# Expert input rows gathered in quarters and turned by one VectorE transpose, with the low part on GpSimd

## Chip, cores and metric
One core of one Trainium2 chip runs the whole program. The metric is the device time of one execution in microseconds; the median of three runs of the kernel before is 2125.86 us (2125.09 to 2127.89).

## What is computed
One inference step of a one-layer encoder: RMSNorm and modulation, a mixer (forgetting attention and a gated linear recurrence), then a mixture of experts, and a last RMSNorm. The change touches only the experts. In numpy terms:

```
h2   (1152 tokens, 1024)          # 1024 prompt tokens and 128 sample tokens
eid  (1152, 2)                    # the two experts of each token, of 32
for each expert e:
    x = h2[tokens of e]           # a block of up to 128 rows
    y = (silu(x @ w1[e]) * (x @ w3[e])) @ w2[e]      # 1024 -> 512 -> 1024
out[token] = sum of its two y, each times its weight
```

All data is float32. Products that must be exact to float32 are made of three products of a faster 32-bit type: each operand is split in a high part (the value copied to that type) and a low part (the value minus the high part), and hi·lo, lo·hi and hi·hi are summed.

## The kernel before, in words
The last block of the program (from line 2245) holds the output projection and routing, then the expert loop, then the combination. Every engine has its own written-out program, and semaphores order them.

**Routing.** TensorE and VectorE make, token tile by token tile, a table in PSUM. From it VectorE writes `rows` (which token row of `h2_d` each of 128 slots of expert s holds) and `dest` (where the result row goes), lines 2704 to 2706, and then counts blocks for experts with over 128 tokens. TensorE ends this stage with `total` (2925) and four matmuls that only keep it busy (`keep_on(4)`, 2965).

**One expert s** (the loop runs over s = 0 to 31, `NE` = 32). Its weights come as six units of 1 MB (u = 0 to 3 for w1 and w3, 4 and 5 for w2), each with a buffer of its own for the raw values and one for the high part; the low part is written over the raw values.
- SyncE's queue (`load_units`, 2276) loads unit u of the next expert as soon as TensorE has done with unit u of this one (semaphore `e_mm`). Its order is units 0 to 3 of s+1, then units 4 and 5 of s.
- GpSimd (2361 to 2368): once TensorE has turned the rows of s, it gathers the rows of expert s+2 into one of two `xg` buffers by one indirect DMA, and then scatters the result rows of expert s-2 by another.
- TensorE (3023 to 3033): `gate_up(s)`, 48 matmuls on units 0 to 3; `turn_rows(s+1)`, eight 128x128 transposes of the gathered rows into PSUM banks 0 and 1 (line 2975); `down(s-1)`, 24 matmuls on units 4 and 5; `turn_hidden(s)`, four transposes.
- ScalarE (2496 to 2519) makes the high part of each unit (2456), the gate's silu, the high part of the turned rows (`put_x`, 2462), the high part of the turned hidden rows, and copies the results out. Its order in step s: `put_h(s-1)`, units 4 and 5 of s-1, silu, units 0 and 1 of s+1, `put_x(s+1)`, unit 2, half of `put_y(s-1)`, unit 3, the other half.
- VectorE (2788 to 2803) makes the low part of each unit (helper at line 456), the low part of the turned rows and of the hidden rows, and `gated` (silu times up, 2770). Its order in step s: `put_h(s-1)`, units 4 and 5 of s-1, unit 0 of s+1, `gated(s)`, `put_x(s+1)`, units 1, 2 and 3 of s+1.
- `gate_up(s+1)` waits for both parts of the turned rows (`xT_A`, `xT_D`, 2996 and 2997).

The feature index of a gathered row is cut as n*8+c: chunk c of the turned tile holds the features n*8+c on partition n. This is what the transposes' stride over `xg` does (`"p (n c) -> p c n"`).

Of the kernel before, what the change touches and what calls it, by code (L numbers as in the profile page):

```python
# [8 lines left out]
U32 = mybir.dt.uint32  # L9
# [4 lines left out]
P = 128  # L14
# [48 lines left out]
def trunk(nc, a, o):  # L63

    (y_p, y_s, k_p, v_p, lf_p, cv_p, h_p, k_s, v_s, lf_s, cv_s, h_s) = o
    with ExitStack() as ctx:
# [288 lines left out]
        def taken(flat):  # L355

            at_ = [0]

            def take(*dims):
                n = 1  # L360
                for d in dims:
                    n *= d
                at_[0] += n
                return view(flat, at_[0] - n, *dims)
            return take
# [15 lines left out]
        oh4, ed, den, pg = rt(NT, GR), rt(NT), rt(NT), rt(NT)  # L381
        iotaf, grp, thr = rt(P), rt(NE), rt(9)
        slotv = rt(1)
        rt = taken(qTs[:].rearrange("p c n -> p (c n)"))
        E = rt(NT, 2, NE)
        M = rt(2, NE)
# [28 lines left out]
        hs, hh_ = view(WR, D * 6, DE), view(WR, D * 6 + DE, DE)  # L415
        hhTh, hhTl = part("hhT_hi", "weights", D * 7, DE // P, P), part("hhT_lo", "weights", D * 7 + DE, DE // P, P)
        gidx, didx = (sb(name, [P, 1], U32) for name in ("gidx", "didx"))

        def place(u, s):

# [1824 lines left out]
        with nc.Block() as block:  # L2245
# [75 lines left out]
            def _(e):  # L2321
# [7 lines left out]
                for r in range(2):  # L2329
                    e.iota(V[:, r], [[P, NT], [TOK * (1 - r), 2]], base=-4 * TOK, channel_multiplier=1, allow_small_or_imprecise_dtypes=True).then_inc(sem("iotas"), 1)  # L2330
                e.memset(g8, -BIG).then_inc(sem("iotas"), 1)

                e.wait_ge(sem("a2"), 2)
                for t in range(NT):
# [10 lines left out]
                        split_mt(j, n + 1)  # L2345

                def gather(s):
                    e.indirect_dma_start(out=xg[s % 2], out_offset=None, in_=h2_d, in_offset=bass.IndirectOffsetOnAxis(ap=rows[:, s:s + 1], axis=0),  # L2348
                                         bounds_check=TOK - 1, oob_is_err=False).then_inc(sem(f"xg_in{s % 2}"), 16)

                def scatter(s):
                    e.wait_ge(sem("yo_A"), 2 * s + 2)
# [4 lines left out]
                e.wait_ge(sem("table"), 1)  # L2357
                gather(0)
                gather(1)
                e.wait_ge(sem("table"), 3)  # L2360
                for s in range(NE):
                    if s + 2 < NE:
                        e.wait_ge(sem("tx_mm"), s + 1)
                        gather(s + 2)
                    if s >= 2:
                        scatter(s - 2)
                scatter(NE - 2)
# [27 lines left out]
            def _(e):  # L2395
# [65 lines left out]

                def put_x(s):
                    e.wait_ge(sem("tx_mm"), s + 1)
                    act(xTh, banks(0, 2).rearrange("p (c n) -> p c n", c=CH), ACT.Copy).then_inc(sem("xT_A"), 1)

                def silu(s):
                    w, n = place(1, s)
# [97 lines left out]
            def _(e):  # L2565
# [138 lines left out]
                ts(rows[:, 0:2], PS[:, 7, 64 + NE:64 + NE + 2], OVER, float(TOK - 1), ALU.add, ALU.min).then_inc(sem("table"), 1)  # L2704
                ts(rows[:, 2:], PS[:, 7, 64 + NE + 2:64 + 2 * NE], OVER, None, ALU.add).then_inc(sem("table"), 1)
                ts(dest, PS[:, 7, 64:64 + NE], OVER, None, ALU.add).then_inc(sem("table"), 1)
                st.wait()
                tt(oh4, g8[:, :, 0:GR], bc(gm[:, :, 0], NT, GR), ALU.subtract).then_inc(sem("gd"), 1)
                tt(ed, em[:, :, 1], em[:, :, 0], ALU.subtract).then_inc(sem("edd"), 1)

                def weigh():
                    e.wait_ge(sem("gexp"), 1)
# [64 lines left out]
                def last_y():  # L2777
                    w, n = place(5, NE - 1)
                    e.wait_ge(sem(f"y_out{(NE - 1) % 2}"), (NE - 1) // 2 * 16)
                    e.wait_ge(sem(f"e_mm{w}"), n + 1)  # L2780
                    copy(yo[(NE - 1) % 2][:, 512:], PS[:, 6, :]).then_inc(sem("yo_A"), 1)
                split(0, 0)
                split(1, 0)
                first_x(0)
# [3 lines left out]
                for s in range(NE):  # L2788
                    if s:
                        put_h(s - 1)  # L2790
                        split(4, s - 1)
                        split(5, s - 1)
                    if s + 1 < NE:
                        split(0, s + 1)
                    if s == 0:
                        split(1, 1)
                    gated(s)
                    if s + 1 < NE:
                        put_x(s + 1)
                        if s:  # L2800
                            split(1, s + 1)
                        split(2, s + 1)
                        split(3, s + 1)
                    else:
                        split(4, s)
                        put_h(s)
                        split(5, s)
                    if s in aside:
                        aside[s]()
# [57 lines left out]
            def _(e):  # L2867
# [55 lines left out]
                    last.then_inc(sem("tab_mm"), 1)  # L2923

                def total():
                    e.wait_ge(sem("table"), 3)
                    e.wait_ge(sem("Mrun"), NT)
                    mm(PS[:, 7, 0:NE], ones[:], Mrun[:, NT % 2, :], start=True, stop=True).then_inc(sem("total_mm"), 1)

                for j in range(2):  # L2930
                    for k in range(2):
# [30 lines left out]
                table(LAST - 1)  # L2962
                table(LAST)
                total()
                keep_on(4)


# [55 lines left out]
                for s in range(NE):  # L3023
                    gate_up(s)
                    if s + 1 < NE:
                        turn_rows((s + 1) % 2, s + 1)
                        if s:
                            down(s - 1)
                    else:
                        down(s - 1, (4,))  # L3030
                    turn_hidden(s)
# [61 lines left out]
```

## Time and profile before
| | us |
|---|---|
| median of three runs | 2125.86 |
| profiled execution | 2124.89 |
| its span, first to last instruction | 2123.2 |
| TensorE busy | 2030.4 (96%) |
| VectorE busy | 1333.8 (63%) |
| ScalarE busy | 1077.3 (51%) |
| GpSimd busy | 387.0 (18%) |

The profile is one execution taken by the hardware profiler. Its page has the busy time of each engine, the span in 40 slices, the DMA queues, the chain of work that ended last and the costliest groups; further views of the same trace give groups by line, waits, stretches of time, and single instructions in order of time. Matmuls are pipelined, and the recorded length of one is longer than its distance to the next; so steps on TensorE are measured here from start to start. The expert loop runs from about 1490 us to about 2075 us of the span.

### The profile page before, as it was taken

To read this page: it belongs to the slowest core of one execution; us is meant where nothing else is said; L and a number is where in the kernel's file an instruction comes from. 1 tells how busy PE (TensorE), PEld (TensorE's weight loads), DVE (VectorE), ACT (ScalarE), POOL (GpSimd) and SP (SyncE) were. 2 spreads that over 40 slices of the span, in tenths; PEclk is the share of its full clock that TensorE was granted. 3 is DMA by queue.
4 is the path that set the end of the run, shared out by engine and by line. 5 is a ranking of instruction groups with operands and counts; after the bars stand their busy time and mean duration, and the time that the engine had idled before them with its cause. 6 is when DMAs were issued, how large, how long until landed. Compare 5 with 4: busy or idle time off the path is not lost. (4 is left out here: it accounts for less than half of the span.)

```text
span 2123.2 us, 30707 instructions
## 1 busy us (share of the span) xinstructions
PE 2030.4 (96%) x11914; PEld 1744.3 (82%) x11914; DVE 1333.8 (63%) x1832; ACT 1077.3 (51%) x1420; POOL 387.0 (18%) x280
## 2 busy tenths in 40 slices
PE   7999999999988999999999999999999999999996
PEld 5888888877655999989999999787788888888882
DVE  5523666665563355574443444477799888888885
ACT  4422444443344355663333333222678777878874
POOL 2101111101011122230010001232112232222315
PEclk9999999999998999999999999998999999999998
DMA  9113222343377111144454486335899999999987
GB/s 295 60 70 97 62 62 62 106 146 124 108 247 216 32 43 42 32 118 141 138 167 140 134 245 186 118 116 196 305 369 372 366 381 384 391 388 389 382 313 278
DMA packets 259347, 415.19 MB, mean 196 GB/s; under 512 B 23948, under 2 KB 200868, under 8 KB 234511
## 3 DMA queue, kind: packets, MB, share of 16 engines
q1 hardware_dynamic: 245858, 382.42, 52.5%
q0 software_dynamic: 10944, 24.01, 3.0%
q10 hardware_dynamic: 2412, 6.94, 0.9%
q8 instruction: 91, 1.49, 0.3%
q14 instruction: 42, 0.34, 0.0%
HBM read 381.87 MB, written 45.66 MB: 201 GB/s over the span
## 5 line engine op out<-in xcount | busy, mean ns | idle before, releaser
L456 DVE TENSOR_TENSOR ew_lo<-region,ew_hi 128x2048 fp32r<-128x2048 f32 x192 | 431.7, 2286 | 25.0 <-ACT ew_hi L2456 24.5
L2456 ACT ACTIVATE ew_hi<-region 128x2048 fp32r<-128x2048 f32 x192 | 367.7, 1918 | 118.2 <-DMA region<-in_w 117.2
L456 DVE TENSOR_TENSOR wm_lo<-weights,wm_hi 128x1024 fp32r<-128x1024 f32 x91 | 124.5, 1370 | 144.6 <-ACT wm_hi L1551 144.0
L2985 PE MATMUL PS<-ew_lo,xT_hi 128*128 128x512 f32 x512 | 202.1, 395 | 7.9 <-issue 6.5
L2987 PE MATMUL PS<-ew_hi,xT_hi 128*128 128x512 f32 x512 | 199.8, 390 | 0.0
L2986 PE MATMUL PS<-ew_hi,xT_lo 128*128 128x512 f32 x512 | 199.3, 389 | 0.0
L1551 ACT ACTIVATE wm_hi<-weights 128x1024 fp32r<-128x1024 f32 x92 | 97.1, 1057 | 130.7 <-DMA weights<-in_w_pa 70.7
L1406 ACT ACTIVATE region<-region,small 128x896 f32<-128x896 f32 (+7 forms) x128 | 98.4, 770 | 83.0 <-DVE small L1706 82.9
L463 PE MATMUL PS<-h_lo,wx_hi 128*128 128x384 f32 x384 | 133.5, 348 | 0.4 <-DVE mixtmp L1803 0.4
L1706 DVE CUSTOM_DVE_ANT_0 region<-PS,region 128x896 f32<-128x896 f32 (+7 forms) x128 | 92.3, 755 | 60.8 <-PE PS L1977 60.0
L463 PE MATMUL PS<-h_lo,wm_hi 128*128 128x384 f32 x384 | 129.1, 336 | 1.1 <-POOL wm_lo L456 1.1
L464 PE MATMUL PS<-h_hi,wx_lo 128*128 128x384 f32 x384 | 129.2, 337 | 0.0
L465 PE MATMUL PS<-h_hi,wx_hi 128*128 128x384 f32 x384 | 129.1, 336 | 0.0
L465 PE MATMUL PS<-h_hi,wm_hi 128*128 128x384 f32 x384 | 128.4, 334 | 0.0
L464 PE MATMUL PS<-h_hi,wm_lo 128*128 128x384 f32 x368 | 122.9, 334 | 0.0
L2985 PEld LDWEIGHTS PS<-ew_lo,xT_hi 128*128 128x128 f32 x512 | 96.2, 188 | 30.0 <-issue 9.6
L2353 POOL DMA_INDIRECT y_d<-weights,slots x32 | 71.9, 2245 | 262.8 <-ACT weights L2485 257.0
L2987 PEld LDWEIGHTS PS<-ew_hi,xT_hi 128*128 128x128 f32 x512 | 96.1, 188 | 20.5
L2986 PEld LDWEIGHTS PS<-ew_hi,xT_lo 128*128 128x128 f32 x512 | 96.2, 188 | 19.2
L2348 POOL DMA_INDIRECT weights<-h_d,slots x32 | 68.1, 2129 | 211.9 <-PE PS L2975 189.4
L3018 PE MATMUL PS<-ew_lo,hhT_hi 128*128 128x512 f32 x248 | 99.3, 401 | 0.0
L3020 PE MATMUL PS<-ew_hi,hhT_hi 128*128 128x512 f32 x248 | 97.0, 391 | 0.0
(454 smaller groups left out, 4887.9 us busy)
## 6 DMA issues: line engine op xcount, KB each, us to landing
region<-in_w SPq DMA_DIRECT2D x192, 1024.0 KB, 7.9
region<-in_w_mod SPq DMA_DIRECT2D x23, 1024.0 KB, 7.5
weights<-in_w_gate SPq DMA_DIRECT2D x46, 512.0 KB, 4.0
weights<-in_w_in SPq DMA_DIRECT2D x36, 512.0 KB, 4.0
weights<-in_w_pb SPq DMA_DIRECT2D x24, 512.0 KB, 3.7
weights<-in_w_pa SPq DMA_DIRECT2D x24, 512.0 KB, 3.7
region<-in_x_prompt SPq DMA_DIRECT2D x16, 512.0 KB, 4.9
region<-F_d SPq DMA_DIRECT2D x16, 512.0 KB, 6.8
```

The costliest lines, as they stand in the source:

```text
L456: return eng.tensor_tensor(lo, x, hi.bitcast(F32), ALU.subtract)
L463: mm(out, lh(c), rl(c), start=c == 0, stop=False)
L464: mm(out, ll(c), rh(c), start=False, stop=False)
L465: last = mm(out, lh(c), rh(c), start=False, stop=c == CH - 1)
L1406: act(row, row, ACT.Exp, scale=-1.0, bias=mn[:, u:u + 1], accum_out=ls[:, u:u + 1]).then_inc(sem(f"exp{hh}"), 1)
L1551: act(wmh[mix_slot[k]], wm[mix_slot[k]], ACT.Copy).then_inc(sem(f"wm_hi{mix_slot[k]}"), 1)
L2456: act(ewh[w], ew[w], ACT.Copy).then_inc(sem(f"eu_hi{w}"), 1)
L2985: mm(out, lh(c), ewl[w][:, c, :], start=first and c == 0, stop=False)
L2986: mm(out, ll(c), ewh[w][:, c, :], start=False, stop=False)
L2987: last = mm(out, lh(c), ewh[w][:, c, :], start=False, stop=end and c == 3)
L3018: mm(out, hi[:, c, :], ewl[w][:, q, :], start=c == 0, stop=False)
L3020: last = mm(out, hi[:, c, :], ewh[w][:, q, :], start=False, stop=c == 3)
```

## The change
For experts from the sixth on (s >= `QUARTERED` = 5):
- GpSimd gathers the rows of an expert by four indirect DMAs of 1 KB per row instead of one of 4 KB. Partition 32q+i gets, in quarter g of the buffer, feature quarter q of the row of slot 32g+i. The indices are 4*row + q, in a new table `rows4`.
- VectorE turns the whole 128x1024 buffer in one instruction that transposes each 32x32 block within its 32 partitions. It reads the buffer with a step of 8 elements and writes `xT_f`, an SBUF tile that lies where the routing's `qTs` was. It comes behind `put_h(s-1)` and ahead of unit 4 of s-1. TensorE's eight transposes are dropped.
- ScalarE's high part reads `xT_f` instead of PSUM, and waits for TensorE's use of the last expert's rows.
- GpSimd makes the low part (`put_x`), behind the four gathers of expert s+3 and ahead of the scatter of s-2; VectorE's is dropped.
- Each gather is issued by the step before (gather s+3 once s+1 has been turned), and `gather(2)` goes ahead of the loop.

Once, ahead of the loop: GpSimd fills `quarter` with four memsets, VectorE makes `rowsf`, TensorE spreads it over the partitions by 16 small matmuls (`quarters`) between `total` and `keep_on(4)`, and VectorE waits for them and makes `rows4` ahead of the first expert's units.

```diff
+        QUARTERED = 5
+        rows4 = sb("rows4", [P, NE, 4], U32)[:]
+        xg4 = [v.rearrange("p (g j c) -> p g c j", g=4, c=CH) for v in xg]
+        xT_f = qTs[:].rearrange("p c n -> p (c n)")
...
                 def gather(s):
-                    e.indirect_dma_start(out=xg[s % 2], out_offset=None, in_=h2_d, in_offset=bass.IndirectOffsetOnAxis(ap=rows[:, s:s + 1], axis=0),
-                                         bounds_check=TOK - 1, oob_is_err=False).then_inc(sem(f"xg_in{s % 2}"), 16)
+                    if s < QUARTERED:
...
+                        return
+                    for g in range(4):
+                        e.indirect_dma_start(out=xg[s % 2][:, 256 * g:256 * (g + 1)], out_offset=None, in_=h2_d.rearrange("t (a n) -> (t a) n", a=4),
+                                             in_offset=bass.IndirectOffsetOnAxis(ap=rows4[:, s, g:g + 1], axis=0),
+                                             bounds_check=4 * TOK - 1, oob_is_err=False).then_inc(sem(f"xg_in{s % 2}"), 16)
+
+                def put_x(s):
+                    e.wait_ge(sem("xT_A"), s + 1)
+                    lo_of(e, xTl, xT_f.rearrange("p (c n) -> p c n", c=CH), xTh).then_inc(sem("xT_D"), 1)
...
                 for s in range(NE):
-                    if s + 2 < NE:
-                        e.wait_ge(sem("tx_mm"), s + 1)
-                        gather(s + 2)
+                    if s + 3 < NE:
+                        e.wait_ge(sem("tx_mm"), s + 2)
+                        gather(s + 3)
+                    if QUARTERED <= s + 1 < NE:
+                        put_x(s + 1)
                     if s >= 2:
                         scatter(s - 2)
...
                 def put_x(s):
                     e.wait_ge(sem("tx_mm"), s + 1)
-                    act(xTh, banks(0, 2).rearrange("p (c n) -> p c n", c=CH), ACT.Copy).then_inc(sem("xT_A"), 1)
+                    turned_ = banks(0, 2)
+                    if isinstance(s, int) and s >= QUARTERED:
+                        w, n = place(3, s - 1)
+                        e.wait_ge(sem(f"e_mm{w}"), n + 1)
+                        turned_ = xT_f
+                    act(xTh, turned_.rearrange("p (c n) -> p c n", c=CH), ACT.Copy).then_inc(sem("xT_A"), 1)
...
+                ts(rowsf, PS[:, 7, 64 + NE:64 + 2 * NE], OVER, None, ALU.add).then_inc(sem("rowsf"), 1)
...
+                e.wait_ge(sem("quarter"), 4)
+                e.wait_ge(sem("rows4_mm"), 1)
+                ts(rows4, PS[:, 7, 128:128 + 4 * NE].rearrange("p (g e) -> p e g", g=4), 4.0, quarter, ALU.mult, ALU.add).then_inc(sem("table"), 1)
...
+                def turn_rows(s):
+                    j = s % 2
+                    e.wait_ge(sem(f"xg_in{j}"), 64 * (s // 2 + 1) - 48 * ((QUARTERED - j + 1) // 2))
+                    e.wait_ge(sem("xT_A"), s)
+                    e.wait_ge(sem("xT_D"), s)
+                    nc.vector.transpose(out=xT_f.rearrange("p (c g n) -> p g c n", c=CH, g=4), in_=xg4[j]).then_inc(sem("tx_mm"), 1)
...
                     if s:
                         put_h(s - 1)
+                    if QUARTERED <= s + 1 < NE:
+                        turn_rows(s + 1)
+                    if s:
                         split(4, s - 1)
                         split(5, s - 1)
...
                     gated(s)
+                    if s + 1 < QUARTERED:
+                        put_x(s + 1)
                     if s + 1 < NE:
-                        put_x(s + 1)
...
+                def quarters():
+                    for g in range(4):
+                        for q in range(4):
+                            last = mm(PS[32 * q:32 * q + 32, 7, 128 + NE * g:128 + NE * (g + 1)], ident[:, 32 * g:32 * g + 32], rowsf, start=True, stop=True)
+                    last.then_inc(sem("rows4_mm"), 1)
...
                 total()
+                quarters()
                 keep_on(4)
...
                     if s + 1 < NE:
-                        turn_rows((s + 1) % 2, s + 1)
+                        if s + 1 < QUARTERED:
+                            turn_rows((s + 1) % 2, s + 1)
```

## Rows read from the trace of the kernel before

**Rows 1.** Stretches: length, busy PE, PEld, DVE, ACT, POOL, clock, DMA share, GB/s.
```profile
1480.00:1490.00 10.00, 8.89 (x19) 4.78 (x18) 6.28 (x14) 0.34 (x2) 4.39 (x2) 0.52 0.95 358
1561.90:2049.50 487.60, 483.49 (x2269) 403.36 (x2269) 430.25 (x257) 385.43 (x298) 121.63 (x52) 1.00 1.00 381
1860.00:1910.00 50.00, 49.46 (x235) 41.26 (x234) 42.63 (x26) 38.89 (x31) 10.40 (x5) 1.00 1.00 391
```

**Rows 2.** TensorE in order of time: start, length, instruction (first matmuls of the steps).
```profile
1797.19 0.48 PE L2985 MATMUL PS<-ew_lo,xT_hi 128*128 128x512 f32 x1
...
1808.20 1.04 PE L2975 MATMUL PS<-ident,weights 128*128 128x128 f32 x8
1808.99 0.48 PE L3018 MATMUL PS<-ew_lo,hhT_hi 128*128 128x512 f32 x1
...
1814.95 0.48 PE L2985 MATMUL PS<-ew_lo,xT_hi 128*128 128x512 f32 x1
```

**Rows 3.** Waits between 1561.9 and 2049.5 us: in total, times, longest.
```profile
ACT ew_hi L2456 <- DMA region<-in_w: 101.2, 121, 2.4
```

**Rows 4.** ScalarE and VectorE in order of time around 1810 us.
```profile
1810.33 1.92 ACT L2456 ACTIVATE ew_hi<-region 128x2048 fp32r<-128x2048 f32 x1 [1.33 <-DMA region<-in_w]
1812.15 1.00 ACT L2464 ACTIVATE xT_hi<-PS 128x1024 fp32r<-128x1024 f32 x1
...
1814.33 6.69 DVE L456 TENSOR_TENSOR ew_lo<-region,ew_hi 128x2048 fp32r<-128x2048 f32 x3
```

**Rows 5.** VectorE by group between 1561.9 and 2049.5 us: count, busy us, mean ns.
```profile
L456 DVE TENSOR_TENSOR ew_lo<-region,ew_hi 128x2048 fp32r<-128x2048 f32 x163 | 366.6, 2286 | 21.6 <-ACT ew_hi L2456 21.2
L456 DVE TENSOR_TENSOR xT_lo<-PS,xT_hi 128x1024 fp32r<-128x1024 f32 x27 | 33.1, 1224 | 35.3 <-ACT xT_hi L2464 35.3
```

**Rows 6.** Two VectorE instructions by line: duration ns min/median/max.
```profile
L2738 DVE TENSOR_TENSOR mixtmp<-mixtmp x1: 195/195/195, 1588.4 to 1588.4; 128x18 f32<-128x18 f32 x1
...
L2649 DVE TENSOR_TENSOR kTs<-kTs x9: 192/193/194, 1375.1 to 1477.9; 128x32 f32<-128x32 f32 x9
```

**Rows 7.** Line 2590 on VectorE alone, then beside a GpSimd subtraction.
```profile
1360.67 1.28 DVE L2590 SCALAR_TENSOR_TENSOR weights<-weights,small,region 128x1024 f32<-128x1024 f32 x1
...
1399.23 3.14 DVE L2590 SCALAR_TENSOR_TENSOR weights<-weights,small,region 128x1024 f32<-128x1024 f32 x1
...
1398.83 2.47 POOL L456 TENSOR_TENSOR ob_lo<-region,h_hi 128x1024 fp32r<-128x1024 f32 x1
```

**Rows 8.** GpSimd's own instructions by line: duration ns min/median/max.
```profile
L2388 POOL TENSOR_TENSOR region<-region x9: 2346/2357/2384, 2086.6 to 2111.7; 128x1024 f32<-128x1024 f32 x9
...
L2348 POOL DMA_INDIRECT weights<-h_d,slots x32: 992/2188/3958, 1483.8 to 2008.2; - x32
```

**Rows 9.** GpSimd gathers and the VectorE subtraction beside each, in order of time.
```profile
1774.44 1.02 POOL L2348 DMA_INDIRECT weights<-h_d,slots  x1 [7.62 <-PE PS L2975]
...
1774.43 2.33 DVE L456 TENSOR_TENSOR ew_lo<-region,ew_hi 128x2048 fp32r<-128x2048 f32 x1 [1.13 <-ACT ew_hi L2456]
...
1827.76 2.98 POOL L2348 DMA_INDIRECT weights<-h_d,slots  x1 [5.87 <-PE PS L2975]
...
1827.56 2.29 DVE L456 TENSOR_TENSOR ew_lo<-region,ew_hi 128x2048 fp32r<-128x2048 f32 x1 [0.64 <-ACT ew_hi L2456]
```

**Rows 10.** Weight loads by SyncE's queue, issue to landing, us min/median/max.
```profile
DMA to landing us min/median/max: 5.0/7.9/11.6
```

**Rows 11.** The start of the loop: TensorE and VectorE; then small matmuls elsewhere.
```profile
1483.11 0.64 PE L2928 MATMUL PS<-mixtmp,ones 128*128 128x32 f32 x2 [0.44 <-DVE slots L2706]
1483.56 6.64 PE L2871 MATMUL PS<-region,ident 128*128 128x512 f32 x8
1490.51 1.16 PE L2975 MATMUL PS<-ident,weights 128*128 128x128 f32 x8 [0.31 <-DMA weights<-h_d,slots]
...
1491.89 1.29 DVE L456 TENSOR_TENSOR xT_lo<-PS,xT_hi 128x512 fp32r<-128x512 f32 x2 [4.24 <-ACT xT_hi L2460]
...
641.78 0.64 PE L2124 MATMUL PS<-region,mixtmp 128*32 128x128 f32 x16
```

More of the change, by code:

```diff
@@ L383, in trunk @@
         slotv = rt(1)
+        rowsf, quarter = rt(NE), rt(1)
         rt = taken(qTs[:].rearrange("p c n -> p (c n)"))
@@ L2331, in _ @@
                 e.memset(g8, -BIG).then_inc(sem("iotas"), 1)
+                e.wait_ge(sem("iotas"), 6)
+                for q in range(4):
+                    e.memset(quarter[32 * q:32 * q + 32, :], float(q)).then_inc(sem("quarter"), 1)
+                e.wait_ge(sem("quarter"), 4)
                 e.wait_ge(sem("a2"), 2)
@@ L2347, in gather @@
                 def gather(s):
-                    e.indirect_dma_start(out=xg[s % 2], out_offset=None, in_=h2_d, in_offset=bass.IndirectOffsetOnAxis(ap=rows[:, s:s + 1], axis=0),
-                                         bounds_check=TOK - 1, oob_is_err=False).then_inc(sem(f"xg_in{s % 2}"), 16)
+                    if s < QUARTERED:
+                        e.indirect_dma_start(out=xg[s % 2], out_offset=None, in_=h2_d, in_offset=bass.IndirectOffsetOnAxis(ap=rows[:, s:s + 1], axis=0),
+                                             bounds_check=TOK - 1, oob_is_err=False).then_inc(sem(f"xg_in{s % 2}"), 16)
+                        return
[6 more added lines that the diff above has]
+                    lo_of(e, xTl, xT_f.rearrange("p (c n) -> p c n", c=CH), xTh).then_inc(sem("xT_D"), 1)
                 def scatter(s):
@@ L2359, in _ @@
                 gather(1)
-                e.wait_ge(sem("table"), 3)
+                e.wait_ge(sem("table"), 4)
+                e.wait_ge(sem("tx_mm"), 1)
+                gather(2)
                 for s in range(NE):
-                    if s + 2 < NE:
-                        e.wait_ge(sem("tx_mm"), s + 1)
-                        gather(s + 2)
+                    if s + 3 < NE:
[3 more added lines that the diff above has]
+                        put_x(s + 1)
                     if s >= 2:
@@ L2709, in _ @@
                 tt(ed, em[:, :, 1], em[:, :, 0], ALU.subtract).then_inc(sem("edd"), 1)
+                e.wait_ge(sem("quarter"), 4)
+                e.wait_ge(sem("rows4_mm"), 1)
+                ts(rows4, PS[:, 7, 128:128 + 4 * NE].rearrange("p (g e) -> p e g", g=4), 4.0, quarter, ALU.mult, ALU.add).then_inc(sem("table"), 1)
                 def weigh():
@@ L2925, in total @@
                 def total():
-                    e.wait_ge(sem("table"), 3)
+                    e.wait_ge(sem("rowsf"), 1)
                     e.wait_ge(sem("Mrun"), NT)
                     mm(PS[:, 7, 0:NE], ones[:], Mrun[:, NT % 2, :], start=True, stop=True).then_inc(sem("total_mm"), 1)
+                def quarters():
+                    for g in range(4):
+                        for q in range(4):
+                            last = mm(PS[32 * q:32 * q + 32, 7, 128 + NE * g:128 + NE * (g + 1)], ident[:, 32 * g:32 * g + 32], rowsf, start=True, stop=True)
+                    last.then_inc(sem("rows4_mm"), 1)
                 for j in range(2):
```

## The prediction
> **What bounds the kernel now.** I began with the busy time in stretches. From 1561.9 us, where expert 4 starts on TensorE, to 2049.5 us, where expert 31 starts, lie 27 steps of the expert loop, as the count of VectorE's `xT_lo` says [rows 1, 5]: 487.60 / 27 = 18.06 us a step. These are the 27 steps that lead to experts 5 to 31, the ones that the change touches. TensorE is busy for 483.5 of the 487.6 us, so it bounds the stage, but the row shows two more resources near their end: VectorE with 430.25 us, 15.94 a step, and DMA with a share of 1.00 at 381 GB/s, 391 at best [rows 1].
>
> TensorE in order of time gives the parts of a step: 48 matmuls of `gate_up` take 1808.20 - 1797.19 = 11.01 us, the eight transposes 0.79 us to the next product, `down` and `turn_hidden` 5.96, in all 17.76 [rows 2]. The mean step is 0.3 longer, since waits creep in. The waits show from where: ScalarE waits 121 times for a weight unit to land, 101 us in all [rows 3]. VectorE waits 35.3 us for the high part of the turned rows and 21.6 us for those of the weights, 2.1 us a step [rows 5]; this is all the idle time it has. The end of a step is a close race: ScalarE waits until 1810.33 for unit 1 of the next expert, then makes the high part of the rows until 1813.15, VectorE the low part until 1814.4, and TensorE is ready for them at 1814.95 [rows 2, 4]. The removed transposes thus sit on an engine that is full, and what replaces them goes to engines and a path with 0.5 to 2.1 us to spare.
>
> **TensorE's part.** The change removes 0.79 us a step, which would leave 17.76 - 0.79 = 16.97 us. TensorE also gets a new wait at the head of `gate_up(s+1)`, for GpSimd; behind it on its queue is everything, so it counts in full if it is late.
>
> **VectorE's part, term by term, per step.**
> - Now 15.94 us of busy time. The low part of the rows goes: 1.22 us [rows 5], of which 0.08 overlaps the next instruction (three subtractions of 2.286 us take 6.69 [rows 4]), so 1.15. Left: 14.79.
> - The 32x32 transpose comes. No row shows one. From below, 1.22 us, the pass over the same 1024 columns in `xT_lo` [rows 5]. It reads with a step of 8 words, though. One instruction does that in the trace: line 2738 reads an operand at that step, 18 columns in 195 ns, while a contiguous one with 32 columns takes 193 [rows 6]. At (2286 - 1224) / 1024 = 1.04 ns a column [rows 5] a contiguous 18 would take 178, so the step costs about 0.93 ns a column, 0.95 us for 1024: 2.17 us. I take 2.17, less 0.08 of overlap: 2.09. One short instruction is thin ground, so the upper end is twice that surcharge, 3.1 us.
> - The low part on GpSimd reads SBUF, and so do both inputs of VectorE's weight subtractions. Line 2590, with two SBUF inputs, takes 1.28 us alone and 3.14 us when it is issued 0.4 us into a GpSimd subtraction of 2.47 us: it ends 1.07 us after that one [rows 7]. VectorE is shut out for the length of the GpSimd instruction, 2.36 us undisturbed [rows 8]. About 0.4 to 0.6 us of it may fall where VectorE would wait for unit 2's high part, whose ScalarE copy (1.92 us) starts behind the 1.00 us for the rows [rows 4]. I take 2.0; the ends are 0 (all in idle time) and 2.4.
> - The indirect DMAs: beside a gather the subtraction took 2.33 instead of 2.29 us [rows 9], so three more cost 0.15.
>
> Sum: 14.79 + 2.09 + 2.0 + 0.15 = 19.03 us a step. VectorE then needs more than the present 18.06 and more than TensorE's 16.97, and becomes the bound: **+0.97 us a step, 27 times, +26 us**. The bounds give 14.79 + 1.14 = 15.9 (then VectorE doesn't bind) and 14.79 + 3.02 + 2.4 + 0.15 = 20.4 (+63).
>
> The rule that speaks against this change is in the Trainium skill, "Vector Engine (DVE) Microarchitecture Reference", section Measured stream behaviour on trn2: a port runs at full rate only over runs of two or more adjacent words. Its figures for single-word steps, 1.71 to 2.51 ns a column, would make an estimate of 1.75 to 2.57 us for the transpose and a step of 18.6 to 19.4 us; the 18-column row agrees with it as far as it goes.
>
> **GpSimd's queue.** It gets three more gathers, the subtraction, and a new order. A gather takes 1.0 us when it meets no subtraction of VectorE [rows 8], but issued at 1827.76, just inside one that ended at 1829.85, it ended at 1830.74, 0.9 us behind it [rows 9]. Issued back to back into back-to-back subtractions, each takes one of them, 2.2 us. The transpose of s+1 is followed on VectorE by units 4, 5 and 0, three subtractions, then `gated` with one SBUF input: the first three gathers end with those, the fourth at about `gated`. Then `put_x(s+1)` waits for the high part and for unit 1's subtraction, and runs 2.36 us. From the end of `gated` this is 0.6 + 2.2 + 2.36 = 5.2 us to the start of `gate_up(s+1)`, and from there 11.0 to the next `gated`: a loop of 16.2 us under a step of 19.0. So GpSimd's wait is covered with 2.8 us left. Its queue is busy for 4 x 2.2 + 3.5 + 2.3 = 14.6 us of 19. The scatter of s-2 now goes about 14 us later, but ScalarE wants it landed one step after; 19 less an issue of 2.3 and a landing of 11.6 at most, as the weight loads have [rows 10], leaves 5. The gathers have two steps to land. All this costs nothing while the cover holds.
>
> SyncE's queue issues what it did. The gathered bytes stay; there are four times the packets, in a stage that leaves DMA some 7% idle (17.6 us of work, worked out below, in 19). ScalarE's copy of the rows costs the same 1.00 us.
>
> **The start, once.** `quarters` is 16 float32 matmuls, two instructions each, ahead of `keep_on(4)`; the transposes of expert 0 come 0.31 us after those, so TensorE is the path there and any delay counts [rows 11]. Where four such 32-column blocks go to four partition quarters, 16 instructions took 0.64 us, about 0.11 per four at full clock; here the clock is 0.52 [rows 1, 11], so 8 x 0.21 = 1.7 us. The ends: 0.9 at full clock, and 32 x 0.23 = 7.4 one after another, as line 2928 has it (0.64 us for two, 0.45 to the next). I take 1.7, nearest to the same form. `rows4` holds back VectorE's first two units, 4.5 us of work, by some 3 us; the 4.24 us that VectorE waits before 1491.89 cover that [rows 11].
>
> **Sum.** 26.2 + 1.7 = +27.9 us on the profiled execution's 2124.89: 2152.8. That execution is 0.97 below the median of 2125.86, so the forecast for the median is 2153 us.
>
> **Rivals.**
> - *VectorE's idle time takes it all, faster.* The subtraction on GpSimd falls beside `gated`, the hidden rows and the 2.1 us of waits, and the transpose runs near 1.2 us. Then DMA is next: 381 x 18.06 = 6.88 MB a step at the best stretch's 391 GB/s are 17.6 us [rows 1], so 27 x -0.46 + 1.7: 2115. For it: the idle time exists. Against: it comes in bits of about 1 us behind ScalarE, not where GpSimd is ready. Chance 0.16.
> - *No change that can be measured* (I count 0.2%, 4.3 us, as that). The transpose is at full rate, the lock costs 2.0: 14.79 + 1.14 + 2.15 = 18.1 us, 2128.5 with the start. Chance 0.10. The Trainium skill, "VectorE: DVE Perf Modes", section Rules for kernel authors, calls the 32x32 transpose fastest on VectorE; with no surcharge for the step, it would give this case.
> - *The path of unit 1.* Step start, half of `gate_up` 5.5, the load 7.7 as between 1802.7 and 1810.33, the copy 1.85, the rows' high part 1.0, the rest of unit 1's subtraction 1.3, GpSimd's 2.4 and 0.1: 19.8 us, +49 in all, 2175. It decides if loads still take over 6.9 us to land. Against: they take 5.0 at best and 7.9 in a full queue [rows 10], and a step of 19 unloads it. Chance 0.13.
> - *GpSimd's queue binds.* If a fourth or later gather misses a gap, `put_x` slips by one or two subtractions; past 2.8 us TensorE starts late, VectorE waits for it at `gated`, and the loop is 16.2 + 4.4 = 20.6 us: +71, 2196. A gather of 3.96 us (two subtractions) is on record [rows 8]. Chance 0.12.
>
> **How the numbers follow.** The forecast keeps 0.49; the slower cases make 0.74 with it, the same 0.10, faster 0.16. The forecast's own range is 2135 to 2172 (transpose 1.6 to 2.9 us). The whole range, 2116 to 2185, leaves out about half of the faster case and the queue case.
>
> **What would show it.** A VectorE transpose group of about 2.2 us x27. VectorE busy or shut out almost all the time: weight subtractions of about 4.4 us, some 27 of them, beside the GpSimd group. TensorE waiting some 2 us a step at line 2985, on GpSimd. DMA share below 1.00. Steps of 19.0 us. If TensorE keeps 99% and steps are under 17.9, the lock and the transpose are mis-sized; if VectorE idles while steps are over 19.5, it is one of the last two rivals. The clock should stay at its upper level; a lower one would be news.

## The result, and the profile after

The kernel after takes 2225.45 us (median of four runs, 2220.8 to 2242.81), the kernel before 2125.52 in the same comparison: a ratio of 1.0482, 95% interval 1.0450 to 1.0514. It is slower, as forecast, but by 100 us where 27 were forecast, and outside the range. The profiled execution took 2223.28 us, its span is 2221.4. Lines have moved: the helper for low parts is 461, the first matmul of `gate_up` 3034, the high part of a weight unit 2479 and that of the rows 2492, the gathers in quarters 2362, the scatter 2372, the transpose on VectorE 2819, `gated` 2802.

The view by stretches (columns as in [rows 1]): first the 27 steps that lead to experts 5 to 31, then one of them in two halves.

```profile
1559.40:2147.80 588.40, 487.77 (x2055) 399.52 (x2054) 486.81 (x257) 386.80 (x298) 382.54 (x156) 0.92 0.83 315
1897.70:1910.00 12.30, 12.29 (x54) 10.19 (x55) 12.30 (x7) 9.20 (x8) 7.45 (x2) 1.00 0.92 354
1910.00:1923.80 13.80, 4.80 (x25) 3.91 (x23) 9.15 (x6) 10.60 (x9) 12.74 (x5) 0.82 0.70 274
```

588.40 / 27 = 21.79 us a step where it was 18.06 [rows 1]: all of the loss is here, 100.8 us. No engine is full. TensorE is busy for 83% of the stretch (99% before), VectorE for 83%, GpSimd for 65%, and the DMA share has fallen from 1.00 to 0.83. So no engine's work is the bound. A chain of waits is, and the view of waits shows its links (what waited, for what, us in total, times, longest):

```profile
ACT ew_hi L2479 <- DMA region<-in_w: 110.8, 104, 2.6
PEld PS L3034 <- issue: 104.1, 26, 9.2
PE PS L3034 <- issue: 99.9, 26, 9.0
POOL weights L2362 <- DVE qTs L2819: 91.6, 24, 6.9
POOL xT_lo L461 <- ACT xT_hi L2492: 83.1, 14, 12.3
DVE ew_lo L461 <- ACT ew_hi L2479: 80.5, 52, 6.7
ACT weights L2499 <- PE PS L3036: 79.3, 14, 10.6
...
DVE qTs L2819 <- POOL xT_lo L461: 20.4, 5, 4.1
```

TensorE waits 99.9 us at the head of `gate_up`, nearly the whole loss; before, this wait came to 4.2 us. The profile puts it down to "issue", but the times show what released it: GpSimd's low part. It ends at 1923.69 in the long step below and the next `gate_up` starts at 1923.79; in the short one it ends at 1944.10 and `gate_up` starts at 1944.20. Of the 27 low parts, 14 waited for ScalarE's high part. The other 13 stood in GpSimd's queue behind the gathers until long after it was ready, and began 17 to 25 us after the step's start. From one `gate_up` to the next, six steps take 26.1 to 27.7 us, two 22.3 and 23.3, then 17 between 19.6 and 21.5 (mean 20.47), and the last two, whose loop passes issue no gather any more, 19.2 and 16.8.

A long step, from 1897.7 to 1923.8, in order of time. GpSimd:

```profile
1897.77 2.90 POOL L2372 DMA_INDIRECT y_d<-weights,slots  x1 [0.16 <-issue]
1905.45 6.73 POOL L2362 DMA_INDIRECT weights<-h_d,rows  x1 [4.78 <-DVE qTs L2819]
1912.48 4.65 POOL L2362 DMA_INDIRECT weights<-h_d,rows  x1 [0.31 <-issue]
1917.44 2.57 POOL L2362 DMA_INDIRECT weights<-h_d,rows  x1 [0.31 <-issue]
1920.31 1.00 POOL L2362 DMA_INDIRECT weights<-h_d,rows  x1 [0.30 <-issue]
1921.34 2.35 POOL L461 TENSOR_TENSOR xT_lo<-qTs,xT_hi 128x1024 fp32r<-128x1024 f32 x1
```

VectorE and TensorE in the same step (the end of a group of x3 or x2 is that of its last instruction):

```profile
1902.49 2.19 DVE L2819 STREAM_TRANSPOSE qTs<-weights 128x1024 f32<-128x1024 f32 x1
1904.61 6.64 DVE L461 TENSOR_TENSOR ew_lo<-region,ew_hi 128x2048 fp32r<-128x2048 f32 x3
1911.18 0.67 DVE L2802 TENSOR_TENSOR weights<-weights,PS 128x512 f32<-128x512 f32 x1
1911.78 4.47 DVE L461 TENSOR_TENSOR ew_lo<-region,ew_hi 128x2048 fp32r<-128x2048 f32 x2
...
1923.82 2.05 DVE L2819 STREAM_TRANSPOSE qTs<-weights 128x1024 f32<-128x1024 f32 x1 [4.08 <-POOL xT_lo L461]
...
1923.79 0.76 PE L3034 MATMUL PS<-ew_lo,xT_hi 128*128 128x512 f32 x1 [9.00 <-issue]
```

The first gather is issued at 1905.45, inside the first of three back-to-back subtractions. It does not end behind that one, at about 1907.8, nor behind the second, but at 1912.18: 0.9 us after the whole chain, when VectorE has gone over to `gated`. The second gather spans the next two subtractions in the same way. The four end at 1921.3, 15.9 us after the first began, and only then comes the low part, though ScalarE had made the high part by 1911.7 (it began at 1910.66 and took 1.04 us). The low part is 9.6 us late, and TensorE's gap is 9.0. A gather with nothing beside it takes 1.00 us (the fourth).

The short step behind it, 1923.8 to 1944.2, shows the other kind: GpSimd, then ScalarE.

```profile
1926.64 2.32 POOL L2362 DMA_INDIRECT weights<-h_d,rows  x1 [1.75 <-DVE qTs L2819]
...
1932.72 1.00 POOL L2362 DMA_INDIRECT weights<-h_d,rows  x1 [0.31 <-issue]
1940.56 3.54 POOL L461 TENSOR_TENSOR xT_lo<-qTs,xT_hi 128x1024 fp32r<-128x1024 f32 x1 [6.83 <-ACT xT_hi L2492]
...
1937.60 1.93 ACT L2479 ACTIVATE ew_hi<-region 128x2048 fp32r<-128x2048 f32 x1 [1.33 <-DMA region<-in_w]
1939.42 1.05 ACT L2492 ACTIVATE xT_hi<-qTs 128x1024 fp32r<-128x1024 f32 x1
```

Here the gathers are through at 1933.7. The low part waits for unit 1 to land (1937.60) and be copied, for the high part of the rows (1940.47), and then for VectorE's subtraction of unit 1 (1939.56 to 1941.85): it takes 3.54 us, of which some 2.35 are its own. That is the path of unit 1. It starts late here: SyncE's queue issues the load of unit 1 at 1931.9, 8.2 us after `gate_up` began, where it is 5.8 in the long step. TensorE's granted clock had fallen in the stall before and `gate_up` began at the lower level. The load itself is short, 5.6 us. Twelve steps with gathers are of this kind, and in eleven of them unit 1 was issued 7.2 to 8.5 us after the start, not 5.8. The groups by line of VectorE and GpSimd in these 27 steps, to hold against [rows 5, 8]:

```profile
L461 DVE TENSOR_TENSOR ew_lo<-region,ew_hi 128x2048 fp32r<-128x2048 f32 x163 | 398.1, 2475 | 80.7 <-ACT ew_hi L2479 80.5
L2819 DVE STREAM_TRANSPOSE qTs<-weights 128x1024 f32<-128x1024 f32 x27 | 57.5, 2129 | 20.4 <-POOL xT_lo L461 20.4
```
```profile
L2362 POOL DMA_INDIRECT weights<-h_d,rows x101 | 233.6, 2313 | 117.9 <-DVE qTs L2819 91.6 <-issue 26.3
L461 POOL TENSOR_TENSOR xT_lo<-qTs,xT_hi 128x1024 fp32r<-128x1024 f32 x27 | 83.1, 3079 | 83.4 <-ACT xT_hi L2492 83.1
```

### The profile page after: what moved, and what is told of

Its sections match the earlier page's. It is cut to its first block and busy times, and to the rows that moved or that the text cites. A ratio compares the mean times of both kernels' runs of the same rounds, so it can differ in the third digit from the quotient of the medians.

```text
span 2221.4 us, 30589 instructions
## 1 busy us (share of the span) xinstructions
PE 2033.5 (92%) x11730; PEld 1740.9 (78%) x11730; DVE 1393.7 (63%) x1834; ACT 1079.0 (49%) x1420; POOL 654.0 (29%) x392
## 5 line engine op out<-in xcount | busy, mean ns | idle before, releaser
L461 DVE TENSOR_TENSOR ew_lo<-region,ew_hi 128x2048 fp32r<-128x2048 f32 x192 | 463.1, 2447 | 85.2 <-ACT ew_hi L2479 84.9
L3034 PE MATMUL PS<-ew_lo,xT_hi 128*128 128x512 f32 x512 | 213.8, 418 | 102.7 <-issue 101.7
L2362 POOL DMA_INDIRECT weights<-h_d,rows x108 | 244.8, 2267 | 141.7 <-DVE qTs L2819 91.6
L3035 PE MATMUL PS<-ew_hi,xT_lo 128*128 128x512 f32 x512 | 210.0, 410 | 0.0
L3036 PE MATMUL PS<-ew_hi,xT_hi 128*128 128x512 f32 x512 | 209.2, 409 | 0.0
L3034 PEld LDWEIGHTS PS<-ew_lo,xT_hi 128*128 128x128 f32 x512 | 103.0, 201 | 128.7 <-issue 106.0
L3036 PEld LDWEIGHTS PS<-ew_hi,xT_hi 128*128 128x128 f32 x512 | 102.5, 200 | 23.0
L3035 PEld LDWEIGHTS PS<-ew_hi,xT_lo 128*128 128x128 f32 x512 | 103.0, 201 | 21.2
L461 POOL TENSOR_TENSOR xT_lo<-qTs,xT_hi 128x1024 fp32r<-128x1024 f32 x27 | 83.1, 3079 | 83.4 <-ACT xT_hi L2492 83.1
```

The lines of the kernel that those rows point to most:

```text
L461: return eng.tensor_tensor(lo, x, hi.bitcast(F32), ALU.subtract)
L2362: e.indirect_dma_start(out=xg[s % 2][:, 256 * g:256 * (g + 1)], out_offset=None, in_=h2_d.rearrange("t (a n) -> (t a) n", a=4), in_offset= ...
L3034: mm(out, lh(c), ewl[w][:, c, :], start=first and c == 0, stop=False)
L3035: mm(out, ll(c), ewh[w][:, c, :], start=False, stop=False)
L3036: last = mm(out, lh(c), ewh[w][:, c, :], start=False, stop=end and c == 3)
```

## The experiments

Twelve kernels were run, in groups that share the runs of the kernel before, and each ratio is to those. "Step" is the mean of the 27 steps that lead to experts 5 to 31 in the profiled execution (18.06 before, 21.79 after).

**a_low_first.** Only the order of GpSimd's queue changes: the low part stands ahead of the gathers.

```diff
                 for s in range(NE):
+                    if QUARTERED <= s + 1 < NE:
+                        put_x(s + 1)
                     if s + 3 < NE:
                         e.wait_ge(sem("tx_mm"), s + 2)
                         gather(s + 3)
-                    if QUARTERED <= s + 1 < NE:
-                        put_x(s + 1)
```

> Queue theory: the loss of the changed kernel comes from GpSimd's queue, where four gathers stand ahead of the low part and each waits for a gap between VectorE's weight subtractions (its first gather takes up to 6.7 us). With the low part issued ahead of the gathers the long steps (23 to 28 us) go and all steps look like the short ones, bounded by unit 1's load, ScalarE's copies and GpSimd's low part: about 19.8 us a step, 2223.3 - 27 x 2.0 = about 2170 us. Overload theory: VectorE's own work and lock-out bound the step; order on GpSimd changes little, over 2210 us. It would also show as VectorE idle under 0.5 us a step.

Measured: 2163.75 us (two runs), ratio 1.0186 (1.0152 to 1.0221), step 19.30. The gathers ahead of the low part cost 2225.45 - 2163.75 = 62 us. What is left above 18.06 has three parts that this run doesn't separate: the path of unit 1 with the subtraction on GpSimd, VectorE shut out while that runs, and a wait that neither the kernel before nor the one after has, ScalarE's for a scatter to land. VectorE's 163 subtractions take 405.0 us where 366.6 were [rows 5]:

```profile
L461 DVE TENSOR_TENSOR ew_lo<-region,ew_hi 128x2048 fp32r<-128x2048 f32 x163 | 405.0, 2530 | 30.2 <-ACT ew_hi L2479 29.9
```

ScalarE's wait for scatters, which stand behind the gathers in GpSimd's queue (total, times, longest):

```profile
ACT weights L2513 <- DMA y_d<-weights,slots: 16.5, 5, 6.1
```

**b_low_vector.** The low part goes back to VectorE, behind `gated`, and reads `xT_f`. The transpose on VectorE and the four gathers stay.

```diff
-                    if QUARTERED <= s + 1 < NE:
-                        put_x(s + 1)
...
-                    lo_of(nc.vector, xTl, banks(0, 2).rearrange("p (c n) -> p c n", c=CH), xTh).then_inc(sem("xT_D"), 1)
+                    turned_ = xT_f if isinstance(s, int) and s >= QUARTERED else banks(0, 2)
+                    lo_of(nc.vector, xTl, turned_.rearrange("p (c n) -> p c n", c=CH), xTh).then_inc(sem("xT_D"), 1)
...
-                    if s + 1 < QUARTERED:
+                    if s + 1 < NE:
                         put_x(s + 1)
...
```

> Low part of the rows back on VectorE, the gathers in quarters and the VectorE transpose kept. Queue theory: nothing waits for GpSimd now except the gathers, which have two steps; VectorE's work is 14.79 + 2.09 + 1.15 + 0.15 = 18.2 us a step, so steps of 18.2 to 18.7 us, 2126 to 2140 us. If the gathers cost by themselves (late landings, DMA contention) or VectorE's in-order waits of 2.1 us come on top of its work, steps of about 20 us, 2175 us.

Measured: 2141.56 (four runs), ratio 1.0091 (1.0060 to 1.0122), step 18.52. Having the low part on GpSimd at all thus costs 22 us more (2163.75 - 2141.56); both kernels have late scatters. The lock-out is gone: the weight subtractions are back at 2.29 us. But gathers are held as before, and the scatter behind them is late. ScalarE waits for it to land in four steps of the 27:

```profile
ACT weights L2511 <- DMA y_d<-weights,slots: 19.1, 4, 7.4
```

**c_one_gather.** One gather of 4 KB a row in place of four; the rest as after. This leaves the quartering out, so the rows of experts 5 to 31 reach the products in another order.

```diff
-                    for g in range(4):
-                        e.indirect_dma_start(out=xg[s % 2][:, 256 * g:256 * (g + 1)], ...)
+                    e.indirect_dma_start(out=xg[s % 2], out_offset=None, in_=h2_d, in_offset=bass.IndirectOffsetOnAxis(ap=rows[:, s:s + 1], axis=0),
+                                         bounds_check=TOK - 1, oob_is_err=False).then_inc(sem(f"xg_in{s % 2}"), 16)
...
```

> Leaves the quartering out: one 4 KB indirect DMA per expert, so the rows of experts 5 to 31 come out in a wrong order; transpose on VectorE and low part on GpSimd stay. Queue theory: one gather is through before the high part is there even when it is starved, so steps of about 19.8 us as with the low part first, 2170 us. If it is the lock-out of VectorE or the low part's own place that costs, it stays over 2205 us; if the four DMAs' landing counts, it falls below the run with the low part first.

Measured: 2163.4 (one run), step 19.43, as with the low part first. One gather can be held over several subtractions too, and it is, but the step has room for one:

```profile
L2361 POOL DMA_INDIRECT weights<-h_d,slots x25 | 106.0, 4241 | 156.0 <-DVE qTs L2817 156.0
```

Its mean of 4.24 us is nearly twice the 2.2 that I had set as the price of one gather; four in a row are what makes the low part late.

**d_none.** Only the set-up ahead of the loop and the new order of gathers and scatter stay; every expert is turned by TensorE.

```diff
-        QUARTERED = 5
+        QUARTERED = NE
```

> No expert is quartered; the set-up (indices, 16 matmuls, VectorE's wait for them) and the new issue order of gathers and scatters stay. Forecast on record: +1.7 us for the set-up, so 2127. The changed kernel's trace speaks for a gain: its expert 0 starts 1.1 us earlier and its first four steps take 67.8 us where the kernel before took 69.2. By that 2123, and more if the new issue order also helps the other 27 steps (17.75 instead of 18.06 would be 2115).

Measured: 2124.23 (12 runs), ratio 0.9990 (0.9971 to 1.0009), step 18.00. Set-up and order cost nothing that can be measured.

**e_halves.** After a_low_first the question was when a gather gets in. If at any end of a subtraction, shorter subtractions let it in sooner. Each weight subtraction on VectorE is cut in two.

```diff
-                    lo_of(nc.vector, ewl[w], ew[w], ewh[w]).then_inc(sem(f"eu_lo{w}"), 1)
+                    lo_of(nc.vector, ewl[w][:, 0:2, :], ew[w][:, 0:2, :], ewh[w][:, 0:2, :]).then_inc(sem(f"eu_lx{w}"), 1)
+                    lo_of(nc.vector, ewl[w][:, 2:4, :], ew[w][:, 2:4, :], ewh[w][:, 2:4, :]).then_inc(sem(f"eu_lo{w}"), 1)
...
```

> The changed kernel with each weight subtraction of VectorE in two halves of 128x1024, nothing else. Boundary theory: a gather is let in only at the end of a subtraction, and misses it when the next is already queued; with ends twice as often, a gather's mean falls from 2.27 to about 1.6 us, the first one's from up to 6.7 to about 3.5, and the low part comes 4 to 5 us earlier in the long steps. The price is 6 x 0.07 us of VectorE a step. Steps of about 19.8 us, 2170 us. If a gather needs a stretch with VectorE off the shared port rather than an end, nothing gets shorter: 2223 to 2235 us.

Measured: 2228.68 (two runs), ratio 1.0487, step 21.68: no gain. The idea that any end will do is wrong. GpSimd, then VectorE, in one step:

```profile
1718.35 6.94 POOL L2362 DMA_INDIRECT weights<-h_d,rows  x1 [8.23 <-DVE qTs L2820]
1725.60 7.06 POOL L2362 DMA_INDIRECT weights<-h_d,rows  x1 [0.30 <-issue]
1732.96 1.00 POOL L2362 DMA_INDIRECT weights<-h_d,rows  x1 [0.30 <-issue]
```
```profile
1717.52 6.85 DVE L461 TENSOR_TENSOR ew_lo<-region,ew_hi 128x1024 fp32r<-128x1024 f32 x6
1724.30 0.67 DVE L2803 TENSOR_TENSOR weights<-weights,PS 128x512 f32<-128x512 f32 x1
1724.90 6.88 DVE L461 TENSOR_TENSOR ew_lo<-region,ew_hi 128x1024 fp32r<-128x1024 f32 x6
```

Six halves in a row hold the gather for as long as three whole ones did. It is through 0.9 us after the chain, whatever the number of ends in it.

**f_filler.** In the kernel after, TensorE's granted clock is at its lower level for 92 of the 588 us, in 14 stretches, and in the kernel before, in the same steps, for none. To see what that is worth, three useless matmuls stand behind `turn_hidden`, where TensorE would wait.

```diff
+                    if s > QUARTERED:
+                        for _k in range(3):
+                            mm(PS[:, 0, :], ident[:], x1b[:, 0, 0:512], start=True, stop=True)
```

> The changed kernel with three matmuls of no use (2.6 us at full clock, into a PSUM bank that is free) in TensorE's stall ahead of gate_up for experts 6 to 31. In the changed kernel 131 of TensorE's matmuls start at the distance of the lower clock level, 27 us more than at the upper. Clock theory: part of the 98 us is that; stalls of 1 to 4 us are then nearly full of work and the granted clock stays up behind them, at least 10 us of the 27 come back, 2213 us or less. Rival: the stalls of 8.9 us, which fillers fill only to a third, make most of the low clock and the fillers delay the short steps by up to 1 us: 2220 to 2240 us.

Measured: 2217.89 (two runs, 2214.94 and 2220.84), ratio 1.0436, step 21.57. The lower level shrank to 47.8 us. The time is 7.6 us lower, between what the two theories gave, but its interval (1.0413 to 1.0459) overlaps that of the kernel after (1.0450 to 1.0514), so a gain is not shown. Either way most of the loss stays: the clock is at most a small part of it, and its share stays open.

**g_alternate** and **h_third.** VectorE turns every second, or every third, expert (from the sixth on), with the low part on VectorE; TensorE turns the others. This asks whether some transposes fit where all don't. The edit shown is h_third's; g_alternate has `s % 2 == 1`.

```diff
+        def quartered(s):
+            return isinstance(s, int) and s < NE and s >= QUARTERED and s % 3 == 2
...
-                    if QUARTERED <= s + 1 < NE:
+                    if quartered(s + 1):
                         turn_rows(s + 1)
...
```

> Only experts 5, 7, ... 31 are gathered in quarters and turned on VectorE; the others go by TensorE as before; the low part is on VectorE throughout. Balance theory: TensorE needs 17.76 and 16.97 us in turn, 17.4 on average, VectorE 15.9 and 18.2, 17.1 on average, so both are under 18.06 and DMA at its best rate allows 17.6: steps of 17.6 to 17.8 us, 2113 to 2119 us, faster than both kernels. Rival: the two kinds of step don't average, since buffers let no engine run ahead, and each long one counts in full (18.5 and 18.0): 2131 us.

Measured: 2129.51 (11 runs), ratio 1.0017 (1.0003 to 1.0031), step 18.19, with ScalarE waiting 14.0 us for scatters.

> As the alternate kernel, but only every third expert (5, 8, ... 29). Balance theory: TensorE 17.5, VectorE 16.7 on average: 17.7 to 17.9 us a step, 2115 to 2121 us. Rival as there: 18.5 for a third of the steps, 18.0 for the rest, 2129 us.

Measured: 2121.33 (10 runs), ratio 0.9984 (0.9970 to 0.9998), step 17.91. This is 0.16% below the kernel before, inside what I count as no change, though its interval, alone of all here, lies wholly below 1.

**i_vector_scatter_first.** As b_low_vector, with GpSimd's scatter ahead of the four gathers, so that nothing which is waited for soon stands behind them.

```diff
                 for s in range(NE):
+                    if s >= 2:
+                        scatter(s - 2)
                     if s + 3 < NE:
...
-                    if s >= 2:
-                        scatter(s - 2)
```

> The kernel with the low part on VectorE, and the scatter of s-2 back ahead of the gathers of s+3 in GpSimd's queue. In that kernel ScalarE waits four times, up to 7.4 us and 19 us in all, for a scatter to land, which the prediction had taken for covered with 5 us left. Theory: four gathers that wait out VectorE's subtractions push the scatter past that cover; with the scatter first these waits go, 18.52 falls to about 17.9 to 18.1 us a step and 2141 to about 2127. Rival: VectorE's 18.2 us of work bind in their place: 2134 or more.

Measured: 2126.62 (10 runs), ratio 1.0012 (0.9996 to 1.0027), step 18.03. ScalarE's wait for the scatter is gone, and so are 15 us. The kernel is level with the one before, though TensorE turns no rows of experts 5 to 31. The first four of the 27 steps and the other 23, columns as in [rows 1]:

```profile
1570.30:1646.70 76.40, 70.56 (x309) 57.58 (x309) 75.95 (x54) 58.07 (x46) 59.13 (x18) 0.98 0.96 357
1646.70:2057.00 410.30, 397.95 (x1748) 322.59 (x1746) 404.91 (x231) 328.23 (x252) 314.67 (x111) 1.00 1.00 386
```

TensorE has room now, 18 us of it, and VectorE has next to none: 99% busy. DMA is as full as before in the 23 steps and less so in the four. The equal means hide two kinds of step. Of the 27, 14 take 17.6 us, which none does in the kernel before (17.7 at least); the first three take 18.9, 18.9 and 21.2, where VectorE also has some 5 us of one-off work of the routing left, and a later one 20.3. The median step is 17.6 us, where it is 18.0 in the kernel before and 17.75 in d_none. So the plain step gets a little shorter, and a few long steps take it back. A kernel that starts them some experts later was not run. The gathers are held for as long as ever (up to 8.2 us each) and nobody minds.

**j_third_scatter_first**, **k_vector_one_gather**, **l_alternate_scatter_first.** The scatter order of i with every third expert, with every second, and, for k, b_low_vector with one gather of 4 KB (the quartering is left out, so the rows of experts 5 to 31 come in another order).

> Every third expert turned on VectorE, low part on VectorE, scatter first. The same theory: the kernel with every third had few such waits, so little is left to gain, 2117 to 2120 us; if VectorE's 16.7 us and TensorE's 17.5 do average, the step falls from 17.91 to 17.75, 2117. Rival: no change, 2121.

Measured: 2126.30 (12 runs), ratio 1.0006 (0.9990 to 1.0022), step 18.14. The small gain of h_third doesn't show here; h_third itself was not run again, so whether it is real stays open.

> Low part on VectorE, scatter behind the gather as in the changed kernel, but one 4 KB gather instead of four of 1 KB (the rows of experts 5 to 31 come out in a wrong order). It leaves of the change only the transpose on VectorE. Theory: the four gathers cost only through the scatter behind them, so this run is as the one with the scatter first, 2125 to 2130 us. Rival: VectorE's added 0.94 us of work is what costs: 2137 to 2142 us, as with four gathers.

Measured: 2126.55 (8 runs), ratio 1.0000 (0.9980 to 1.0019), step 18.10. Four gathers instead of one cost nothing once nothing waits behind them.

> Every second expert turned on VectorE, low part on VectorE, scatter first. Its kernel with the scatter last showed three waits of ScalarE for a scatter, 14 us in all, 0.5 us a step. Theory: these go, 18.19 falls to 17.7, 2116 us, faster than both kernels by 0.4%. Rival: the two kinds of step don't average, 2125 to 2130.

Measured: 2128.24 (12 runs), ratio 1.0020 (1.0006 to 1.0034), step 18.03.

In sum, from 2225 to 2164 by moving the low part ahead of the gathers (62 us), to 2142 by taking it off GpSimd (22), to 2127 by moving the scatter ahead of the gathers (15). What remains of the change then is level with the kernel before. No version was shown to beat that by the 0.2% that I count. Not run was the order with the low part still on GpSimd, but low part and scatter both ahead of the gathers.

## Why the prediction was wrong, and where it held

- **The step that failed** is "each takes one of them, 2.2 us: the first three gathers end with those, the fourth at about `gated`", and with it "GpSimd's wait is covered with 2.8 us left". Gathers took 2.31 us on average, close to the 2.2, but the mean hides what decides: 6.7, 4.65 and 2.6 us for three in a row in the long step. The one long gather that I had, 3.96 us [rows 8], I used only in a rival; no row showed four gathers in a row. In the eight longest steps the run of four ended 20 to 25 us after the step began, with the high part ready at 13.8 to 17.0. The cover wasn't 2.8 us but less than nothing, and a_low_first priced it at 62 us.
- **The rivals, at 0.12 and 0.13, were what happened, in turn.** The long steps are GpSimd's queue (predicted 20.6 for every step; eight steps of 22.3 to 27.7 came, and five of the other 17 had a late queue too). The 12 with gathers that waited for the high part are the path of unit 1, worked out as 19.8 and measured at 19.6 to 21.5. In the short step above its terms read: start to unit 1 landed 13.8 us (5.5 + 7.7 = 13.2 predicted), copy 1.85, high part 1.0, wait and low part together 3.6 (1.3 + 2.4 predicted). That the sum agrees is luck, since its terms are off in both directions. The loads did get shorter, as I had argued against this rival (median 6.1 us where it was 7.9 [rows 10], 5.6 here); what made up for that is `gate_up` at the lower clock after a stall, 8.2 us to the issue where I had 5.5. So the two are not alternatives: the queue's stall makes the next step's path longer. In the last step, with no gather and the clock at its upper level throughout, the same path is through at 16.3 us.
- **VectorE as the bound at 19.03 us** never was. It was busy or shut out 486.81 / 27 = 18.0 us a step and idle for the rest. Term by term: the transpose was right (2.13 us measured, 2.17 predicted). The lock-out was a little over half its size: the subtractions ran over 2.286 us by 30.8 us in all, 1.14 a step, where 2.0 was taken; 39.8 us, 1.5 a step, in a_low_first. With low part and transpose both on VectorE its terms add to 14.79 + 1.15 + 2.09 = 18.03. That i_vector_scatter_first, where VectorE does fill the step, has a mean step of 18.03 is in part luck: 17.6 us in its plain steps, and over 18.9 in the first three.
- The estimate from the Trainium skill's "Vector Engine (DVE) Microarchitecture Reference", Measured stream behaviour on trn2, was 1.75 to 2.57 us; this trace agrees, at 2.05 to 2.21 us.
- **TensorE's part** was right as a removal (the transposes are gone) and worthless as a gain. In i_vector_scatter_first it is free for 18 us of 487 and the kernel isn't faster. In its first four steps VectorE holds, with DMA at 0.96; in the plain ones of 17.6 us both are full, and which of the two holds them was not told apart.
- **The scatter's cover of 5 us** was wrong too: a_low_first shows ScalarE waiting up to 6.1 us for one to land, b_low_vector up to 7.4. I had priced the gathers ahead of it at 2.3 us each there as well.
- **The start** was taken at +1.7 us and cost nothing that can be measured (d_none). From `total` to the first `gate_up` it is 9.33 us now (1482.31 to 1491.64) and was 9.57 ([rows 11] have the start of it). The 16 small products are 32 instructions in 0.66 us, and the next group starts 0.58 us after they do:

```profile
1482.31 0.64 PE L2970 MATMUL PS<-mixtmp,ones 128*128 128x32 f32 x2 [0.54 <-DVE kTs L2735]
1482.88 0.66 PE L2975 MATMUL PS<-kTs,ident 128*32 128x32 f32 x32
1483.46 6.28 PE L2913 MATMUL PS<-region,ident 128*128 128x512 f32 x8
```

- **The clock** was expected to stay up. It fell (0.92 over the stage, 0.82 in the second half of the long step), 14 times, each time in or right behind a stall of 2.1 to 9.3 us (from the start of the last instruction before it to the start of `gate_up`).
- **A slip in the sums.** By its own terms the forecast's range for a transpose of 1.6 to 2.9 us is 2138 to 2173, not 2135 to 2172. Nothing hangs on it.

The direction was right, and three of the signs named in advance came true: a transpose group of 2.1 us, a DMA share under 1.00, and TensorE waiting at the head of `gate_up` (3.7 us a step, where 2 was named). Three did not: steps of 19.0 us, VectorE busy almost all the time, and some 27 subtractions of about 4.4 us (21 took over 2.5, and they average 3.8). The mark "VectorE idles while steps are over 19.5: one of the last two rivals" is the one that identified the case.

## What to carry to other kernels

An indirect DMA issued by GpSimd doesn't cost its mean beside a VectorE that subtracts back to back from SBUF. Price it by its longest, since it can be held until VectorE does something else (6.7 us here for 1.0). So put nothing that another engine waits for soon behind a row of them, and work out a queue's cover with the worst case of its head. And before taking work from a full engine, add up the others: in i_vector_scatter_first TensorE, VectorE and DMA stood within 3% of one another once the work had moved (0.96, 0.99, 0.99), and no version gained more than could be measured.

## What was not expected of the hardware

**When a gather gets in.** I followed GpSimd's indirect DMAs in the five kernels with whole subtractions (after, a, b, c, f). Taken were those issued inside a VectorE subtraction that has two SBUF inputs and another such one right behind it, and each was followed over every such end that it met. At the first end, waiting under 2.4 us, it got in 236 times of 299. Once it had missed one and waited longer, it got in at 3 of 57 later ends; otherwise it stayed out until the chain was over. In e_halves it got in at 70 of 87 ends in its first 1.2 us and at none of 55 after; it did get in twice later, where VectorE left about 0.1 us between two halves. At a first end, the wait before it mattered: all 89 that had waited 1.6 to 2.4 us got in, and 57 of 104 that had waited 1.2 to 1.6. In the kernel after, the transposes put the first gather right there (0.8 us after the transpose's end, 1.4 us before the end of the subtraction that it falls in), and the same step takes 20 us where the gather gets in and up to 26 where it doesn't. The longest wait of all made a GpSimd DMA of 1.0 us one of 8.25 (a gather in l_alternate_scatter_first). VectorE loses next to nothing by it (2.29 us a subtraction in b).

The Trainium skill, "SBUF — State Buffer", section Who interferes with whom, says that issue order decides who blocks and that the second to issue is blocked until the first finishes. The runs agree for GpSimd's subtraction: the low part issued at 1940.56, inside a subtraction of VectorE, ended 2.25 us after that one. For its indirect DMAs they show more, a wait over up to three subtractions that were issued after it, and over five halves in e_halves. What decides it inside the chip no run here shows.

**The clock follows the waits.** In the kernel after, each of the 14 stretches at the lower level (1.2 GHz, 92 us in all) came with a stall of TensorE of 2.1 to 9.3 us, and reached into the next step. There 131 matmuls came at half their rate, 27 us more than at the upper level. That is an upper estimate of its cost, through the loads too, which are issued as `gate_up` frees their buffers. In f_filler, which halved the time at the lower level, the time was 7.6 us lower, and the intervals of the two kernels overlap.
